# A two-block transformer step on one core: the second block's input projection runs on the residual before its norm root is known, and VectorE scales each result tile by the root row

## The reference

```python
def rmsnorm(x, g):                     # xf * rsqrt(mean(xf * xf) + EPS) * g, mean over the 1024 channels
# first_block ends:
lat = lat + g2 * conv_ffn(hl, ffn_w_up, ffn_conv_w, ffn_conv_b, ffn_w_down)   # D_FF = 2816
x = rmsnorm(lat, final_g)
# second_block begins:
h = rmsnorm_2(x, pre_mix_norm)
proj = h @ w_in                        # 1024 x 5888
q_r, k_r, v_r, g_r, q_s, k_s, v_s, gate_r, gate_s = jnp.split(proj, SPLIT_IDX, axis=-1)
ret = silu(g_r) * retention_chunkwise(q_r, k_r, v_r)     # 4 heads, 128 / 256 wide
swa = swa_gqa_sinks(q_s, k_s, v_s, sinks)                # 8 heads, 64 wide
merged = sigmoid(gate_r) * (ret @ w_ret_out) + sigmoid(gate_s) * (swa @ w_swa_out)
x = x + rmsnorm_2(merged @ w_out, post_mix_norm)
```

## Time and profile before

| | |
|---|---|
| time, median of 3 runs | 934.34 us (933.89 to 934.79) |
| time of the profiled execution | 934.09 us |
| its span, first to last instruction | 932.0 us |
| PE busy | 905.9 us, 97% of the span |
| DVE busy | 645.0 us, 69% |
| ACT busy | 508.1 us, 55% |
| mean granted clock | 0.993 of full |

### The profile page before, as it was taken

The page is one execution under the profiler, slowest core; times in us unless marked ns, Lnnn a source line. Parts: engine busy times, 40 slices in busy tenths (PEclk is TensorE's granted clock), DMA queues, the critical chain, the costliest instruction groups (busy, mean ns, idle before and its releaser), DMA issues.

```text
span 932.0 us, 17009 instructions
## 1 busy us (share of the span) xinstructions
PE 905.9 (97%) x6294; PEld 824.3 (88%) x6294; DVE 645.0 (69%) x1036; ACT 508.1 (55%) x798; POOL 24.0 (3%) x22
## 2 busy tenths in 40 slices
PE   6799999999999999999999999999999999999997
PEld 2468888888899999999999898999999799999996
DVE  4968488888887677767667866774466766555555
ACT  6552366666665665555555655545454565444443
POOL 0720000000000000000000000000000000000000
PEclk9899999999999999999999999999999999999999
DMA  8569663334335266555655343344445446555551
GB/s 307 180 229 330 256 214 126 134 133 133 134 111 166 71 209 198 184 179 179 192 174 170 122 156 134 136 159 159 161 155 204 159 158 213 192 182 180 183 188 56
DMA packets 45437, 160.92 MB, mean 173 GB/s; under 512 B 5200, under 2 KB 6608, under 8 KB 45264
## 3 DMA queue, kind: packets, MB, share of 16 engines
q1 hardware_dynamic: 43632, 156.56, 49.2%
q10 hardware_dynamic: 1760, 3.74, 1.1%
HBM read 159.23 MB, written 1.05 MB: 172 GB/s over the span
## 4 chain that ended last, share of the span: by engine, by line
PE 92%; DVE 2%; POOL 2%; ACT 1%; DMA 1%; issue 0%; SPq 0%; DVEq 0%; ACTq 0%
PE bank L420 22%; PE bank L421 21%; PE bank L422 21%; PE bank L1133 4%; PE bank L486 4%; PE bank L488 4%; PE bank L487 4%; POOL tok L1523 1%; PE bank L1194 1%; PE bank L1147 1%; PE bank L1236 1%; PE bank L1216 1%; PE bank L1232 1%; DMA tok<-in_tok 1%; PE bank L1166 1%; DVE w_lo L414 1%
## 5 line engine op out<-in xcount | busy, mean ns | idle before, releaser
L414 DVE TENSOR_TENSOR w_lo<-raw,w_hi 128x1024 fp32r<-128x1024 f32 x260 | 317.0, 1233 | 153.2 <-ACT w_hi L407 152.9
L420 PE MATMUL bank<-h_hi,w_hi 128*128 128x256 f32 (+1 forms) x1248 | 372.5, 298 | 1.9 <-DVE h_lo L602 0.6
L422 PE MATMUL bank<-h_hi,w_lo 128*128 128x256 f32 (+1 forms) x1248 | 366.8, 294 | 0.0
L421 PE MATMUL bank<-h_lo,w_hi 128*128 128x256 f32 (+1 forms) x1248 | 366.3, 293 | 0.0
L407 ACT ACTIVATE w_hi<-raw 128x1024 fp32r<-128x1024 f32 x260 | 269.7, 1051 | 110.4 <-PE bank L422 74.4
L420 PEld LDWEIGHTS bank<-h_hi,w_hi 128*128 128x128 f32 x1248 | 235.5, 189 | 12.1 <-issue 3.6
L421 PEld LDWEIGHTS bank<-h_lo,w_hi 128*128 128x128 f32 x1248 | 235.3, 189 | 6.4
L422 PEld LDWEIGHTS bank<-h_hi,w_lo 128*128 128x128 f32 x1248 | 234.0, 188 | 5.8
L420 PE MATMUL bank<-y_hi,w_hi 128*128 128x256 f32 x304 | 86.4, 284 | 0.0
L421 PE MATMUL bank<-y_lo,w_hi 128*128 128x256 f32 x304 | 85.9, 282 | 0.0
L422 PE MATMUL bank<-y_hi,w_lo 128*128 128x256 f32 x304 | 85.7, 282 | 0.0
(11 more groups left out here) (250 smaller groups left out, 1121.2 us busy)
## 6 DMA issues: line engine op xcount, KB each, us to landing
raw<-in_stream SPq DMA_DIRECT2D x260, 512.0 KB, 3.8
arena<-in_ada SPq DMA_DIRECT2D x24, 512.0 KB, 5.7
xres<-in_ada SPq DMA_DIRECT2D x8, 512.0 KB, 3.3
tok<-in_tok SPq DMA_DIRECT2D x4, 512.0 KB, 9.4
con<-in_con ACTq DMA_DIRECT2D x1, 1472.0 KB, 9.7
xres<-in_tok ACTq DMA_DIRECT2D x1, 1024.0 KB, 9.0
out<-arena SPq DMA_DIRECT2D x4, 256.0 KB, 2.1
arena<-in_post_mix ACTq DMA_DIRECT2D x1, 512.0 KB, 4.2
```

What stands on the lines that cost most here:

```text
L414: dve.tensor_tensor(w_lo[c.slot][:, :], raw[c.slot][:, :], w_hi[c.slot][:, :].bitcast(F32), ALU.subtract).then_inc(S("split_lo"), 1)
L420: pe.matmul(dst, hi_w, a_hi, start=start, stop=False, skip_group_check=True)
L421: pe.matmul(dst, hi_w, a_lo, start=False, stop=False, skip_group_check=True)
L422: return pe.matmul(dst, lo_w, a_hi, start=False, stop=stop, skip_group_check=True)
```

## The change

* The last two hidden tiles are multiplied interleaved (`row_tiles_last`): output tiles 0 to 3 of the one, then 0 to 3 of the other, then both for each of 4 to 7. A PSUM bank is so finished earlier relative to the end.
* ACT makes the high part of the projection's input directly from the residual, times the channel gain (`scaled_hi`), alternating with the squares. DVE makes the low part (`scaled_lo`). The root is not in it, and `norm_input` with its L592 and L600 is gone from this seam.
* PE runs the first two projection tiles on it at once, all high-input matmuls first and the low-input ones after (`first_columns_late`), then the two sums of squares, then the other tiles. The 10 bridging matmuls are gone here.
* DVE now takes every projection tile out of PSUM, multiplied by the root row (`evacuate` moved from ACT to DVE). ACT applies the sigmoid afterwards, SBUF to SBUF (`gate_sigmoid`), and `silu` comes one step later.
* The residual is scaled by its final root in steps 6 to 13 of the loop and no longer in 0 to 7.
* Some semaphores are merged into others (`exps`, `distances`, the two steps of each root), which adds some register arithmetic to the head loop of the first block.

```diff
+        def row_tiles_last(pe, chunks, banks, acts):
...
+            pe.wait_ge(S("split_lo"), chunks[0].n + 1)
+            for m in range(4):
+                tile(0, m)
+            pe.wait_ge(S("split_lo"), chunks[1].n + 1)
+            pe.wait_ge(S("u_lo"), JF)
+            for m in range(4):
+                last = tile(1, m)
+                if m % 2 == 1:
+                    last.then_inc(S("bank_done"), 1)
+            for m in range(4, KT):
+                for i in range(2):
+                    last = tile(i, m)
...
+        def scaled_hi(act, update, m):
+            x = slice(m * T, m * T + T)
+            wait_residual(act, update, m)
+            act.activation(h_hi[:, x], xres[:, x], ACT.Copy, scale=final_pre[:, m:m + 1]).then_inc(S("h_hi"), 1)
+
+        def scaled_lo(dve, q, m):
+            x = slice(m * T, m * T + T)
+            dve.wait_ge(S("h_hi"), (q + 1) * KT + m + 1)
+            dve.scalar_tensor_tensor(h_lo[:, x], xres[:, x], final_pre[:, m:m + 1], h_hi[:, x].bitcast(F32), ALU.mult,
+                                     ALU.subtract).then_inc(S("h_lo"), 1)
...
-            square_residual(act, 1)
-            norm_rstd(act, 1, dst=final_rstd)
-            norm_rstd(act, 2, bank=6, eps=eps_sq)
-            split_h_hi(act, 2)
...
+            for m in range(KT):
+                scaled_hi(act, 1, m)
+                x = slice(m * T, m * T + T)
+                act.activation(wide[:, x], xres[:, x], ACT.Square).then_inc(S("norm_squares"), 1)
+            hi(act, Chunk(N_IN2, AHEAD))
+            norm_rstd(act, 1, 3, bank=6, eps=eps_sq)
+            norm_rstd(act, 2, 3, dst=final_rstd)
...
+            def gate_sigmoid(t):
+                act.wait_ge(S("in2_copied"), t + 1)
...
-            for t in range(JF - 2, JF):
-                ffn_down(t, t % 4, Chunk(N_IN2 - JF + t), False, t == JF - 1)
-            norm_sum(pe, 1)
-            weighted_sum(pe)
-            keep_clock(pe, LOW_BANKS[0], IDLE)
+            pe.wait_ge(S("u_lo"), JF - 1)
+            row_tiles_last(pe, [Chunk(N_IN2 - JF + t) for t in (JF - 2, JF - 1)], LOW_BANKS,
+                           [(y_hi[:, s * T:s * T + T], y_lo[:, s * T:s * T + T]) for s in ((JF - 2) % 4, (JF - 1) % 4)])
...
                 if t == 0:
-                    first_columns(pe, [Chunk(N_IN2), Chunk(N_IN2, 1)], [psum[0][:, 0:T], psum[1][:, 0:T]], 3 * KT)
+                    pe.wait_ge(S("residual"), KT + 4)
+                    first_columns_late(pe, [Chunk(N_IN2), Chunk(N_IN2, 1)], [psum[0][:, 0:T], psum[1][:, 0:T]], 3 * KT)
+                    norm_sum(pe, 1)
+                    weighted_sum(pe)
...
-            add_product(dve, lambda m: mod[:, 5 * KT + m:5 * KT + m + 1], 1, N_IN2, LOW_BANKS,
-                        lambda m: add_weighted_squares(dve, m))
...
-            dve.wait_ge(S("norm_rstd"), 3)
-            norm_input(dve, 2, lambda m: final_pre[:, m:m + 1])
-
+            add_product(dve, lambda m: mod[:, 5 * KT + m:5 * KT + m + 1], 1, N_IN2, LOW_BANKS)
+            for m in range(KT):
+                scaled_lo(dve, 2, m)
+            lo(dve, Chunk(N_IN2, AHEAD))
+            for m in range(KT):
+                add_weighted_squares(dve, m)
+            def evacuate(t):
+
+                if t == 0:
+                    dve.wait_ge(S("norm_rstd"), 2 * 2)
+                dve.wait_ge(S("multiplied"), N_IN2 + t + 1)
...
+                dve.tensor_tensor(dst, psum[t % IN2_BANKS][:, 0:T], rstd[:, 0:T], ALU.mult).then_inc(S("in2_copied"), 1)
...
-                if t < TILES_IN2:
+                if 1 <= t < TILES_IN2:
                     lo(dve, Chunk(N_IN2, t + AHEAD))
-                if t < KT:
-                    scale_residual(dve, t)
+                for old in (() if t < 2 else (0, 1) if t == 2 else (t - 1,)):
+                    evacuate(old)
+                if RESIDUAL_FIRST <= t < RESIDUAL_FIRST + KT:
+                    scale_residual(dve, t - RESIDUAL_FIRST)
```

More of the change, by code:

```diff
@@ L119 @@
 IDLE = 10
+E_QD, E_QE, E_KE, E_KD = 1, 4, 5, 6
 TURN_BANKS = (6, 7, 4, 5)
@@ L126 @@
 X_FIRST = T_GR + 6
+RESIDUAL_FIRST = 6
 SWA_FIRST = T_QR
@@ L475, in row_tile, with tile @@
             last.then_inc(S("multiplied"), 1)
+        def row_tiles_last(pe, chunks, banks, acts):
+            def tile(i, m):
+                a_hi, a_lo = acts[i]
+                return three(pe, psum[banks[m // 2]][:, (m % 2) * T:(m % 2) * T + T], chunks[i].slot,
+                             slice(m * P, m * P + P), a_hi, a_lo, False, i == 1)
+            pe.wait_ge(S("split_lo"), chunks[0].n + 1)
[10 more added lines that the diff above has]
+                    last = tile(i, m)
+                    if m == KT - 1:
+                        last.then_inc(S("multiplied"), 1)
+                if m == 5:
+                    last.then_inc(S("bank_done"), 1)
         def row_tokens(pe, chunks, banks, acts, first, stop):
@@ L528, in keep_clock, with norm_rstd @@
                 pe.matmul(psum[bank][:, 0:P], ones, ones, start=True, stop=True, skip_group_check=True)
-        def norm_rstd(act, k, bank=7, dst=rstd[:, 0:T], eps=eps):
-            act.wait_ge(S("norm_summed"), k + 1)
-            act.activation(dst, psum[bank][:, 0:T], ACT.Ln, scale=1.0 / D, bias=eps).then_inc(S("norm_log"), 1)
-            act.wait_ge(S("norm_log"), k + 1)
+        def norm_rstd(act, k, summed, bank=7, dst=rstd[:, 0:T], eps=eps):
+            act.wait_ge(S("norm_summed"), summed)
+            act.activation(dst, psum[bank][:, 0:T], ACT.Ln, scale=1.0 / D, bias=eps).then_inc(S("norm_rstd"), 1)
+            act.wait_ge(S("norm_rstd"), 2 * k + 1)
             act.activation(dst, dst, ACT.Exp, scale=-0.5).then_inc(S("norm_rstd"), 1)
@@ L582, in split_h_hi, with norm_input @@
                 x, dst = normed[:, m * T:m * T + T], h_hi[:, m * T:m * T + T]
-                if shift is None:
-                    act.activation(dst, x, ACT.Copy).then_inc(S("h_hi"), 1)
-                else:
-                    act.activation(dst, x, ACT.Identity, bias=shift(m)).then_inc(S("h_hi"), 1)
-        def norm_input(dve, q, gain, shift=None):
+                act.activation(dst, x, ACT.Identity, bias=shift(m)).then_inc(S("h_hi"), 1)
+        def scaled_hi(act, update, m):
[7 more added lines that the diff above has]
+                                     ALU.subtract).then_inc(S("h_lo"), 1)
+        def norm_input(dve, q, gain, shift):
             behind = 2
@@ L746, in _ @@
             act.wait_ge(S("cc_in"), 16)
-            act.activation(cs, cc[:, :], ACT.Silu).then_inc(S("cs"), 1)
-            act.wait_ge(S("cs"), 1)
+            act.activation(cs, cc[:, :], ACT.Silu).then_inc(S("cs_hi"), 1)
+            act.wait_ge(S("cs_hi"), 1)
             act.activation(cs_parts[:, :, 0:2], cs_pairs, ACT.Copy).then_inc(S("cs_hi"), 1)
@@ L778, in _ @@
                     act.wait_ge(S("eps"), 1)
-                    act.activation(rstd, psum[1][:, :], ACT.Ln, scale=1.0 / D, bias=eps).then_inc(S("tok_log"), 1)
-                    act.wait_ge(S("tok_log"), 1)
+                    act.activation(rstd, psum[1][:, :], ACT.Ln, scale=1.0 / D, bias=eps).then_inc(S("tok_rstd"), 1)
+                    act.wait_ge(S("tok_rstd"), 1)
                     act.activation(rstd, rstd, ACT.Exp, scale=-0.5).then_inc(S("tok_rstd"), 1)
@@ L850, in out_rstd @@
                 act.wait_ge(S("o_summed"), h + 1)
-                act.activation(o_rs, total, ACT.Ln, scale=1.0 / P, bias=eps).then_inc(S("o_log"), 1)
-                act.wait_ge(S("o_log"), h + 1)
+                act.activation(o_rs, total, ACT.Ln, scale=1.0 / P, bias=eps).then_inc(S("o_rstd"), 1)
+                act.wait_ge(S("o_rstd"), h * 2 + 1)
                 act.activation(o_rs, o_rs, ACT.Exp, scale=-0.5).then_inc(S("o_rstd"), 1)
@@ L957, in _ @@
             log_exp_tables(act)
-            square_residual(act, 1)
-            norm_rstd(act, 1, dst=final_rstd)
-            norm_rstd(act, 2, bank=6, eps=eps_sq)
-            split_h_hi(act, 2)
-            def evacuate(t):
-                act.wait_ge(S("multiplied"), N_IN2 + t + 1)
-                z = psum[t % IN2_BANKS][:, 0:T]
-                dst = in2_dst(t)
-                if dst is not None:
-                    act.activation(dst, z, ACT.Copy).then_inc(S("in2_copied"), 1)
-                elif t < T_GR:
-                    v = v_index(t)
-                    if v >= 2:
-                        act.wait_ge(S("v2_turned"), v - 1)
-                    act.activation(v_tmp[v % 2], z, ACT.Copy).then_inc(S("in2_copied"), 1)
-                elif t < T_GS:
-                    act.activation(gate_dst(t), z, ACT.Sigmoid).then_inc(S("g_sigmoid"), 1)
+            for m in range(KT):
[7 more added lines that the diff above has]
+                act.wait_ge(S("in2_copied"), t + 1)
+                if t < T_GS:
+                    g = t - T_GR
+                    if g < 2:
+                        act.wait_ge(S("v2_turned"), 9)
+                    else:
+                        act.wait_ge(S("g_silu"), g - 1)
```

(7 more changed lines are left out.)

81 lines of the change are left out of this document (39 added, 42 removed).

## The result

The changed kernel took 935.88 us (median of 22 runs, 933.36 to 937.00); the kernel before, run beside it on the same chips, 933.78 us. The ratio is 1.0019, with a 95% interval of 1.0012 to 1.0025. That is a loss of about 1.8 us, just inside the 0.2% that I had called no change, and 0.9 us above the 935.0 us forecast. The profiled execution took 936.42 us, with a span of 934.6 us. Times alone did not say which of my cases it was. The traces do.

The account below looks back on a forecast made before the run. PE was taken to bound the kernel, busy 97% of the span. A 7 us head start, all given back, left +0.7 us at tile 3 and other terms about 0: 934.8, forecast 935.0 us, range 933.9 to 937.4.

Parts of the forecast that it names:

- The sum: At the start of projection tile 3: 529.0 against 528.27, +0.7 us, the whole head start given back.
- Tail: Last two hidden tiles: PE waits 1.1 us for the last one, nothing on the path waits, counted 0.
- ACT's pairs: Scaled rounding plus square on ACT at the seam: 0.75 us a pair, eight take 6.0, done at 515.7.
- Weighted squares: Eight on DVE after its low inputs, each waiting for the one before: 4.6 us, ending at 522.6.
- Roots, chunk, two splits, bank: Before tile 3: ACT's roots then chunk, DVE's two splits, then tile 0's bank freed; PE stands about 2.9 us.
- The new work of DVE: Projection loop: 46 multiplications of 0.42 us, some 15 to 19 us more on DVE, hidden by PE.
- DVE becomes late: Rival, chance 0.10: DVE's loop work makes PE wait 1 to 2 us near 626, giving 936 to 937.
- first rival: Clock lost in the new gap before tile 3, chance 0.35: 1.7 us more, 936.7, or 3.4 more, 938.4.
- wrong if the clock falls: Sign against the prediction: granted clock falling in 510 to 535, around the seam and tile 3.
- likeliest case: The forecast itself, 935.0 us with the clock kept, given 0.45 and a range of 934.2 to 935.8.
- idle time anyway: 0: Seam: removing the 10 bridging matmuls on PE was counted as costing 0.
- ACT loses 46 copies and keeps 24 sigmoids: 0, since ACT waited: Projection loop: moving the PSUM copies off ACT was counted as 0 for the time.

Follow-up runs that it names:

- e_fill: Changed kernel with ten bridging matmuls put back on PE, between projection tiles 2 and 3; 934.81 us, ratio to before 1.0009.
- b_no_keep: Kernel before without its ten bridging matmuls at the seam; 936.21 us, ratio to before 1.0019.
- e_no_tail: Changed kernel with the old order of the tail's matmuls; 935.70 us, ratio to before 1.0019.
- e_hi_early: Changed kernel with ACT's rounding of the chunks of tiles 3 and 4 put ahead of the two roots; 931.68 us, ratio to before 0.9973.
- e_hi_dve: As e_hi_early, with DVE's weighted squares also in turn with its low inputs; 931.81 us, ratio to before 0.9976.
- e_all: As e_hi_dve, with PE's sum-of-squares matmuls also in turn with the first projection matmuls; 929.97 us, ratio to before 0.9962.

## Why the prediction was right, and where it was not

**The sum.** The change's price without the clock is 0.7 us: 189.40 and 189.41 against 188.69, from two kernels. The prediction said +0.7 us, but that agreement is luck. It put all of it at the start of tile 3, where 0.12 was measured (0.22 from the second matmul on). The other 0.50 arises at the loop's exit, which the prediction put at nothing.

**Term by term**, with `y_lo` as zero (0.51 us later in this trace):

* Tail: 1.1 us of wait forecast, 1.01 measured, and hidden as said.
* ACT's pairs: forecast 0.75 each and done at 515.7; measured 5.66 us for eight (510.22 to 515.88), 0.71 each, done at 515.4 on the old zero. The page ScalarE: Activation LUTs of the Trainium skill, section What ACT_TABLE_LOAD costs, gave the basis for an estimate of 5.7 us. The trace agrees with it: its two steps are 0.40 and 0.31, where I had taken 0.42 and 0.33 from rows.
* Tiles 0 and 1: forecast done at 518.0, measured 517.7. Weighted squares: forecast ended 522.6, PE resumed at 522.1. Tile 2: forecast 523.2, measured 522.5. PE's wait for the sum: 1.0 and 0.8.
* Roots, chunk, two splits, bank: the order and the releaser (L1927) as said, 2.9 us of standing forecast, 2.70 measured. Tile 3: forecast 529.0, measured 528.4 on the old zero.
* The new work of DVE: 14.1 us more busy time, and no wait of PE in the loop. Just before the exit's wait the changed kernel is 1.70 us late (its matmul at 693.76), which is 0.22 and the 1.48 of the clock. The rival "DVE becomes late" did not happen at 626 or anywhere before the exit.

**What failed.** First, the choice between forecast and first rival. I gave the loss of the clock 0.35 and the kept clock 0.45. The clock fell in the profiled execution, and by the prediction's own list of signs ("wrong if the clock falls") its likeliest case did not hold. The times of `e_fill` suggest that it falls in most executions. The price of one loss was forecast as 1.7 us; it is 190.88 - 189.41 = 1.47, which is the 16 matmuls of the slow stretch at 0.21 instead of 0.12. The lack was in the evidence: the opening had one wait of 4.30 us and one of 1.08 us, and 2.9 lay between. Taking the bridging matmuls as "idle time anyway: 0" was true of the time they fill and not of what they protect, which `b_no_keep` measured: 1.0019.

Second, the step "ACT loses 46 copies and keeps 24 sigmoids: 0, since ACT waited". It counted ACT's work and not the hop that the change puts in front of it. Inside the loop three banks hide the hop; at the exit nothing does, and it cost 0.50 us.

So 935.88 us is inside the range of 933.9 to 937.4, at the edge of what the likeliest case alone allowed (934.2 to 935.8), and it came about by the first rival in most executions. The budget of the stretch is 0.22 at tile 3, 0.50 at the exit and 1.47 for the clock, 2.19 in all; the first two are read from starts inside the traces, the third is the difference of two stretches. Times and stretches agree elsewhere too: over the seven variants of the changed kernel whose trace has the clock full and whose gap is 1.26 us or less, the difference to before by the ratio less that by the stretch lies between -0.5 and +0.8 us, mean 0.05. The 1.8 us by the ratio then fit 0.7 plus a lost clock in some three quarters of the executions (1.1 / 1.47). The interval of the ratio, 1.1 to 2.3 us, allows anything from a quarter to all of them; the share is worked out and not counted, since the granted clock at that place was read only in profiled executions.

The mean granted clock of each execution, which is on record, points to most or all. One such loss, 3.4 us at half of full, lowers the mean of a span of 934 us by 0.0018. The mean over the executions is 0.9931 for the changed kernel, 0.9939 for `e_no_tail` and 0.9928 for `b_no_keep`, the three with an open gap, and 0.9956 and 0.9957 for the kernel before, timed beside the last two. `e_fill` and `e_hi_early` have 0.9956 and 0.9955. The three lie 0.0017 to 0.0028 lower, a loss in nearly every execution or more. This is no count either: the kernels without such a gap differ among themselves too, from 0.9948 to 0.9966, and the traces show losses in the opening in differing number.

## What to carry to other kernels

A root taken off the input's path does not vanish; look for the first thing that needs it, here the first bank to be reused, and then for what stands in front of it on each in-order engine. Work that needs nothing late, as the two chunks here, belongs ahead of the wait, not behind it: that single move made a gain out of the loss (1.0019 to 0.9973). Two chains of nearly the same length must be shortened together, as `e_hi_dve` and `e_all` show. When a filler is removed, ask how long the gap is in the new order and whether the clock outlives it. And when work moves to another engine, check the last turn of the loop, where the slack of the buffers is no longer there.

## What the runs showed of the hardware

* The loss of the fast clock after an idle gap of 2.7 us is not certain: granted 0.50 for some 3.4 us after gaps of 2.70 and 2.75, full after one of 2.71 and one of 1.26. Where it fell, it did so only some 0.4 to 0.7 us after PE had started again.
* Executions of one program differ by up to 2.8 us at the point where the last hidden tile is ready (504.23 to 507.01 in the nine traces of the changed kernel and its variants), while the stretch behind it repeats to 0.01 us in kernels that should agree (188.69 and 188.69; 189.40 and 189.41). A difference of 0.1 us can be read from one trace if it is taken from a common event and not from the span.
* A 128x256 step on DVE that needs the result just before it comes every 0.59 us (seven in 4.02, the last 0.48 long), one that doesn't every 0.40 (516.85 to 517.24).
* An idle time of PE in the profile understates what it costs, since matmuls overlap: at the exit 0.35 us of idle time delayed what follows by 0.61 (a step of 0.63 and one of 0.22, where both are 0.12 otherwise).
